# Five head norms summed in four row groups with their reciprocals spread by TensorE, and a new order in the attention loop

## The reference

```
def l2norm(t):                                    # DeltaNet q and k, 4 heads of 128 channels each
    return t * rsqrt(sum(t * t, axis=-1) + EPS)
y_dn = (rmsnorm(o_dn, onorm_g) * silu(z)) @ w_dn_out      # over the 128 channels of a head

def merge(r, m, rg, mo):                          # retention and mLSTM, 8 heads of 64 channels each
    r = _rmsnorm(r, ret_norm_w)   * silu(rg)
    m = _rmsnorm(m, mlstm_norm_w) * sigmoid(mo)
    return concatenate([r, m], axis=-1) @ w_out

k = _rmsnorm(_heads(k, 4), k_norm_w)              # attention keys, 4 heads of 64 channels
s_win = q @ k.T * scale       # 16 heads, query blocks of 128, window of 128 on both sides
s_ctx = q @ kc.T * scale      # all context keys
p = softmax([s_win, s_ctx] with one sink logit per head)
y = (p_win @ v + p_ctx @ vc) @ w_out
```

## Time and profile before

| | |
|---|---|
| median of 3 runs | 1986.92 us (1984.42 to 1987.09) |
| the profiled execution | 1981.02 us, of which the span of the trace is 1978.9 us |
| mean granted TensorE clock | 0.96 of full speed |
| PE busy | 1835.8 us (93%), 14672 matmuls |
| PEld busy | 1573.4 us (80%) |
| DVE busy | 918.0 us (46%), 1693 instructions |
| ACT busy | 759.8 us (38%), 1314 instructions |
| POOL busy | 462.2 us (23%), 226 instructions |
| DMA | 261.6 MB, mean 132 GB/s |

### The profile page before, as it was taken

One profiled execution on the slowest core, in us unless ns is written; L12 is line 12 of the kernel. 1 busy time (PEld: TensorE's weight loads), 2 busy tenths in 40 slices (PEclk: granted clock), 3 DMA queues, 4 the chain that ended last, 5 costly groups with the idle time before them and its releaser, 6 DMA issues.

```text
span 1978.9 us, 34373 instructions
## 1 busy us (share of the span) xinstructions
PE 1835.8 (93%) x14672; PEld 1573.4 (80%) x14672; DVE 918.0 (46%) x1693; ACT 759.8 (38%) x1314; POOL 462.2 (23%) x226
## 2 busy tenths in 40 slices
PE   5998999989799999998899969999999989999999
PEld 3777897877689998886687747888888767579998
DVE  1648626566443333435775664222232246744333
ACT  3454522332345454331533233322222234655443
POOL 0235212121123432121230001121212212013343
PEclk7999998999899999999998989999999999999999
DMA  8443344222365545312120023332332336134553
GB/s 319 163 160 128 107 150 150 88 108 87 128 249 186 188 171 184 110 69 96 64 86 23 22 106 108 148 106 107 107 128 107 106 139 228 71 118 181 181 182 128
DMA packets 36581, 261.58 MB, mean 132 GB/s; under 512 B 4048, under 2 KB 4176, under 8 KB 6224
## 3 DMA queue, kind: packets, MB, share of 16 engines
q1 hardware_dynamic: 36432, 259.40, 36.2%
HBM read 258.34 MB, written 1.05 MB: 131 GB/s over the span
## 4 chain that ended last, share of the span: by engine, by line
PE 79%; DVE 11%; ACT 4%; issue 3%; DMA 2%; POOL 1%; SPq 0%; DVEq 0%; ACTq 0%
PE ps L820 18%; PE ps L821 18%; PE ps L822 18%; PE ps L871 2%; PE ps L847 2%; PE ps L837 1%; DVE msq L2415 1%; PE ps L838 1%; PE ps L1089 1%; PE ps L839 1%; PE ps L1077 1%; PE ps L879 1%; PE ps L934 1%; PE ps L1095 1%; PE ps L1416 1%
## 5 line engine op out<-in xcount | busy, mean ns | idle before, releaser
L738 POOL TENSOR_TENSOR wl<-raw,wh 128x1024 fp32r<-128x1024 f32 (+1 forms) x179 | 427.2, 2389 | 1310.1 <-ACT wh L1458 1310.1
L820 PE MATMUL ps<-h_hi,wh 128*128 128x256 f32 (+1 forms) x1696 | 556.6, 328 | 6.9 <-POOL wl L738 4.7
L821 PE MATMUL ps<-h_lo,wh 128*128 128x256 f32 (+1 forms) x1696 | 548.5, 323 | 0.0
L822 PE MATMUL ps<-h_hi,wl 128*128 128x256 f32 (+1 forms) x1696 | 548.1, 323 | 0.0
L1458 ACT ACTIVATE wh<-raw 128x1024 fp32r<-128x1024 f32 (+1 forms) x330 | 342.1, 1040 | 399.9 <-PE ps L822 288.4
L820 PEld LDWEIGHTS ps<-h_hi,wh 128*128 128x128 f32 x1696 | 326.6, 193 | 36.5 <-POOL wl L738 8.9
L821 PEld LDWEIGHTS ps<-h_lo,wh 128*128 128x128 f32 x1696 | 326.4, 192 | 26.1 <-issue 2.7
L822 PEld LDWEIGHTS ps<-h_hi,wl 128*128 128x128 f32 x1696 | 326.4, 192 | 23.9
L1960 DVE TENSOR_TENSOR wl<-raw,wh 128x1024 fp32r<-128x1024 f32 (+1 forms) x151 | 188.1, 1245 | 242.8 <-ACT wh L1458 231.6
L820 PE MATMUL ps<-gh,wh 128*128 128x256 f32 (+1 forms) x528 | 169.3, 321 | 0.0
L822 PE MATMUL ps<-gh,wl 128*128 128x256 f32 (+1 forms) x528 | 168.2, 319 | 0.0
(11 more groups left out here) (414 smaller groups left out, 2741.7 us busy)
## 6 DMA issues: line engine op xcount, KB each, us to landing
raw<-in_mod SPq DMA_DIRECT2D x72, 1024.0 KB, 4.9
raw<-in_ffn_in SPq DMA_DIRECT2D x66, 1024.0 KB, 4.8
raw<-in_ffn_out SPq DMA_DIRECT2D x24, 1024.0 KB, 4.8
raw<-in_w_in SPq DMA_DIRECT2D x16, 1024.0 KB, 4.8
raw<-in_w_gate SPq DMA_DIRECT2D x12, 1024.0 KB, 4.9
raw<-in_w_ab SPq DMA_DIRECT2D x12, 1024.0 KB, 4.9
raw<-in_ffn_out SPq DMA_DIRECT2D x12, 768.0 KB, 4.2
raw<-in_w_at SPq DMA_DIRECT2D x5, 1024.0 KB, 4.8
```

Of the source, the lines that this page charges most:

```text
L738: nc.gpsimd.tensor_tensor(wl[e % SPLIT][:, 0:entries[e]["words"]], part(e), wh[e % SPLIT][:, 0:entries[e]["words"]].bitcast(F32), ALU.subt ...
L820: nc.tensor.matmul(b[:, cols], wh[e % SPLIT][:, w], xh(k), start=(k == 0), stop=False)
L821: nc.tensor.matmul(b[:, cols], wh[e % SPLIT][:, w], xl(k), start=False, stop=False)
L822: ins = nc.tensor.matmul(b[:, cols], wl[e % SPLIT][:, w], xh(k), start=False, stop=(k == nk - 1))
```

## The change

Head norms. `group_sums` replaces the matmul of 512 columns by four matmuls with a stationary matrix of 32 columns, each on 128 tokens, into four row groups (partitions 0 to 31, 32 to 63, ...) of columns 0 to 127 of one bank. Token 128 g + t then stands in column t of row group g. ACT's root and DVE's reciprocal work on 128x128. `group_spread` brings the reciprocals back to 128 x 512 with four matmuls of 128x128 (eight of 128x64 where a tile holds two heads), whose stationary operand is one column of the identity, broadcast, into a PSUM tile of its own (`l2s`, `osp`, `rsp`, `msp`, `aksp`); DVE's product reads it there. These 20 tiles are new in the plan. ACT's waits for `qk_ready`, `rout_ready` and `mout_ready` before a root or square go; PE gets waits for the reciprocals (`l2_inv`, `o_inv`, `rsp_inv`, `msp_inv`, `k_inv`), and where it used to wait for `qk_ready` it waits until `l2s` 7 is evacuated.

Attention loop. PE's order in a round is now transposes of u-1, outputs of u-2, scores of u+1, spread of u-1. `aol` is made by POOL; DVE waits for it before it overwrites `otmp`.

```
--- before.py
+++ after.py
+RETENTION_NORM = ((), (("rss", 0),), (("rss", 1), ("rsp", 0), ("rss", 2)), (("rsp", 1), ("rss", 3), ("rsp", 2)))
+MLSTM_NORM = ((("mss", 0), ("mss", 1), ("msp", 0)),
+              (("mss", 2), ("msp", 1), ("mss", 3), ("msp", 2), ("msp", 3)))
...
+        for w_ in range(16):                                             # POOL
+            pool.wait_ge(sem("ao_hi"), w_ + 1)
+            o = slice(P * (w_ % 2), P * (w_ % 2) + P)
+            nc.gpsimd.tensor_tensor(aol[:, w_ // 2, o], otmp[:, w_ % 2, :], aoh[:, w_ // 2, o].bitcast(F32),
+                                    ALU.subtract).then_inc(sem("ao_lo"), 1)
...
+        def group_sums(key, w, src):                                     # PE
+            b = begin(*key)
+            for g in range(4):
+                ins = nc.tensor.matmul(b[32 * g:32 * g + 32, 0:P], w, src[:, P * g:P * g + P], start=True, stop=True,
+                                       skip_group_check=True)
+            close(ins)
+        def group_spread(key, src, heads=1):
+            b = begin(*key)
+            for g in range(4):
+                rows = (slice(0, P),) if heads == 1 else HALF
+                for e, h in enumerate(rows):
+                    r = 32 * g + 16 * e
+                    ins = nc.tensor.matmul(b[h, P * g:P * g + P], ident[:, r:r + 1].to_broadcast([P, h.stop - h.start]),
+                                           src, start=True, stop=True)
+            close(ins)
...
-                        close(nc.tensor.matmul(begin("l2", m), CA("ones"), sqr[:, m % 2, :], start=True, stop=True))
+                        group_sums(("l2", m), CA("ones")[:, 0:32], sqr[:, m % 2, :])
+                        if m > 0:
+                            pe.wait_ge(sem("l2_inv"), m)
+                            group_spread(("l2s", m - 1), l2c[:, (m - 1) % 2, :])
...
-            b = begin("oss", i)
-            close(nc.tensor.matmul(b, CA("mean_128"), vbf(i), start=True, stop=True))
+            group_sums(("oss", i), CA("mean_128")[:, 0:32], vbf(i))
         for m in range(5, KD):
             hdense(("g0", m), LAT)
+            if m == 5:
+                for i in range(2):
+                    pe.wait_ge(sem("o_inv"), i + 1)
+                    group_spread(("osp", i), B["kd"][:, i, 0, :])
...
         for i in range(8):
             hdense(("aq", i), LAT)
+            if i == 0:
+                for z in range(2):
+                    pe.wait_ge(sem("k_inv"), z + 1)
+                    group_spread(("aksp", z), ars[:, z, 0:P], 2)
...
-                        if m >= 2:                                       # ACT, l2
-                            act.wait_ge(sem("qk_ready"), m - 1)
-                        free(A(l2r[:, m % 2, :], bank("l2", m), ACT.Sqrt, bias=eps), "l2", m)
+                        free(A(l2c[:, m % 2, :], bank("l2", m)[:, 0:P], ACT.Sqrt, bias=eps), "l2", m)
...
-                        act.wait_ge(sem(rdy), i - 1)                     # ACT, rss and mss
+                        full(act, ssname, i - 2)
...
         def l2norm(m):                                                   # DVE
-            evacuated(dve, "l2", m)
-            link(V.reciprocal(l2r[:, m % 2, :], l2r[:, m % 2, :]))
-            V.scalar_tensor_tensor(qk[:, m, :], qk[:, m, :], P ** -0.5 if m < 4 else 1.0, l2r[:, m % 2, :],
-                                   ALU.mult, ALU.mult).then_inc(sem("qk_ready"), 1)
+            if m < 8:
+                evacuated(dve, "l2", m)
+                V.reciprocal(l2c[:, m % 2, :], l2c[:, m % 2, :]).then_inc(sem("l2_inv"), 1)
+            if m > 0:
+                i = m - 1
+                full(dve, "l2s", i)
+                free(V.scalar_tensor_tensor(qk[:, i, :], qk[:, i, :], P ** -0.5 if i < 4 else 1.0, bank("l2s", i),
+                                            ALU.mult, ALU.mult), "l2s", i)
...
-        head_gain(mout, "mss", S("mn"), "mout_ready")
+        for i in range(5):
+            if i < 4:
+                head_root("mss", "msp", i)
+            if i > 0:
+                head_gain(mout, "msp", S("mn"), "mout_ready", i - 1)
...
-        for u in range(16 + 3):                                          # DVE, attention
+        for u in range(16 + 2):
...
-            if u >= 3:
-                w_ = u - 3
-                dve.wait_ge(sem("ao_hi"), w_ + 1)
-                o = slice(P * (w_ % 2), P * (w_ % 2) + P)
-                V.tensor_tensor(aol[:, w_ // 2, o], otmp[:, w_ % 2, :], aoh[:, w_ // 2, o].bitcast(F32),
-                                ALU.subtract).then_inc(sem("ao_lo"), 1)
...
+                if w_ >= 2:
+                    dve.wait_ge(sem("ao_lo"), w_ - 1)
                 free(V.tensor_tensor(otmp[:, w_ % 2, :], bank("ao", w_)[:, 0:P], rinv[:, w_ % 2, :], ALU.mult),
```

172 lines of the change are left out of this document (108 added, 64 removed).

## The result

| | before | changed |
|---|---|---|
| median | 1987.01 us (4 runs, 1984.42 to 1989.12) | 1969.92 us (4 runs, 1968.28 to 1974.38) |
| ratio | | 0.9918, 95% interval 0.9897 to 0.9939 |
| profiled execution / span | 1981.02 / 1978.9 us | 1968.28 / 1966.5 us |
| mean granted clock | 0.961 | 0.961 |

A forecast was written before the change was run, and what follows sets the result against it. PE was taken to bound most of the span (79% of the chain of waits), DVE 11%. Terms −11.5, −5.3, −6, −0.5, +1 and +1.2 sum to −21.1: 1959.9 us profiled, 1966 as median; whole range 1952 to 1982.

The forecast's parts named there:

- The sum, −21.1: Whole kernel: six stage terms together take 21.1 us off the profiled 1981.0, giving 1959.9, or 1966 as median.
- mLSTM norm, −11.5: mLSTM norm: shorter DVE reciprocals and fewer waits start `abo` 11.5 us sooner, PE's new work hidden; bounds −9 and −13.
- Loop, −5.3: Attention loop: round falls from 3.75 to 3.35 us, 0.40 over 13 full rounds, 5.3 us; bounds 0.5 and 7.2.
- The ring: Attention loop: scores, masking, reciprocal, spread, outputs, `otmp` wait on each other; outputs ahead of scores cut this, round 0.40 shorter.
- Retention, −6: Retention norm: PE's 6.98 us gap before `mv` nearly closes, then POOL's `wl` is late; 6 us less, bounds −2 and −8.
- l2, −0.5: l2 norms: PE's added work and one 1.7 us stall nearly cancel DVE's savings; −0.5 us, bounds −4 and +4.
- DeltaNet output +1: DeltaNet output norm: spreads hold PE some 4 us, mostly swallowed by old idle time; +1 us, bounds −1 and +4.
- keys +1.2: Attention keys: spreads wait for reciprocals behind DVE's `wl`; +1.2 us, bounds 0 and +2.5.
- PE's price of a tile, 0.65: All 20 norm tiles: PE pays 0.65 us more each, 0.15 of it for array-shape changes; 13 us; bounds 0 and 0.8.
- A: Rival, whole kernel: spreads are bare, PE's added work paid everywhere but the mLSTM norm; −7.5 us, or 1979; chance 0.2.
- B: Rival, attention loop: POOL's `aol` locks out DVE's small sums, round back to 3.75; total −15.8, 1971; chance 0.1.
- C: Rival, norms: late DVE reciprocals hold PE at the spreads, l2 +10; kernel +5 us slower, or 1992; chance 0.08.

The follow-up runs named there:

- the kernel with only the new order: Kernel before with only TensorE's new order in the attention loop, `aol` staying on DVE and the norms old; run once, 1977.44 us.
- the doubled spreads: Changed kernel with every matmul of the 20 spreads executed twice, the same result written again; run once, 1968.53 us.

## Why the prediction was right

**The sum, −21.1.** The six stages gave −16.0. That this is near is luck in part: the mLSTM norm gave 5.2 us less and the loop 1.3 less than forecast, and the retention norm 3.1 more, some 2 of which are the clock's.

**mLSTM norm, −11.5.** Measured −6.3. The mechanism was right: DVE's work fell by 9.8 us, and `abo` came sooner by 9.7 in two kernels. That the stage gained 11.1 and 11.0 there, near 11.5, is luck in part, since 1.4 of it is before's half clock behind the start of `abo`, which the forecast had kept for its bound of −13. The step said "PE has nothing else here, so all its new work is hidden". That sentence failed. In one of these kernels DVE waits 3.2 us inside the norm where 0.9 was counted, 1.9 of it for the third sum, which stands behind the modulation; and at half clock, spreads of 1.98 and modulation of 1.9 to 2.8 are no longer hidden behind a DVE that needs 2.35 per tile. I had counted the end of before's half clock as a possible gain ("−13") and not the half clock of the new kernel as a loss, though the scan's end has a wait of 2 us in both. That wait stands in the kernels with full clock there too, so what puts the half clock on the norm in one profile and not in another stays open.

**Loop, −5.3.** (13 × 0.40 is 5.2.) Measured −4.0, and by the order alone. The ring was cut as said, PE is the bound as said, but a round is 3.48 and not 3.35. The term that was mis-sized is PE's own: the spread takes 0.37 where it took 0.27, the outputs 1.02 where they took 0.97 and the transposes 1.03 where 1.0 was counted, less 0.08 for scores of 1.06 in place of 1.14. Spread and outputs, both with 64 stationary columns, no longer stand side by side, and I had taken both from the old neighbours; that this is why they take longer is read from the durations and was not tested by itself. 13 × 0.13 = 1.7 us too much, of which the loop's ends gave back 0.4. That `aol` would cost nothing was right; that it brings nothing either I had put as "DVE's 2.75", which bound nothing.

**Retention, −6.** Measured −8.3 to −9.1 in all seven profiles with these norms and single spreads: just outside the bound of −8. Against the kernel with only the new order, which lacks the half clock at 949.6 too, it is −7.4 for the changed kernel, inside it. Mechanism right; next late was nothing (L858 follows the spread at once), where I had left room for POOL's `wl`.

**l2, −0.5.** Measured −0.6, with one stall of 2.15 at the tile that was named by its cause. But −2.4 in the kernels in which no half clock followed the stall, and −1.9 to +1.1 with the old norms: that the number was met says little.

**DeltaNet output +1, keys +1.2.** Measured +1.6 and +2.4 in the first profile. In the four other profiles with the same code in these stages and single spreads the output norm gave +1.4 to +3.1 and the keys +0.1 to +1.5. Both stalls stood where they were put; at the output the spreads were ready earlier than in the forecast (2.32 us of wait for some 4), and the load followed 1.5 later (525.76 after 524.25), near the +1 that I had said.

**PE's price of a tile, 0.65.** The l2 pair went from 6.61 to 7.18: 0.57.

**Rivals.** A (bare spreads) is right for l2, output and keys, where the doubled spreads show it in full, and mostly for retention (2.8 us of some 3.7); it is wrong in what it made of the gain, 3 us for retention and 0.5 for the loop where 9.1 and 4.0 were measured. B (POOL holds DVE) is refuted: the round is 3.48 us with `aol` on DVE (only TensorE's order) and on POOL alike, and in the trace `aol` runs from 1704.30 to 1704.76 while DVE masks from PSUM, and the DVE operations with two SBUF operands (1705.06 on) come later. The lock that the Trainium skill describes (SBUF — State Buffer, "SBUF: two separate sides") thus had nothing to act on here, while in the l2 stage the trace agrees with it once more: 2.48 us for a convolution product, 0.49 without POOL. C was right about the place, one stall at the l2 reciprocals and one at the output, and 2 us each in place of 7 and 4.

The Trainium skill, TensorEngine Tiling (Array Packing), Key Properties, says that changing the tiling mode drains TensorE. The loop's trace agrees in that the spread lets the next matmul begin after 0.37 us with another shape behind it and after 0.27 with its own; no run here isolates the drain, and none shows the 0.15 us that the prediction added per tile. I had weighed it against the norms and not against the loop.

## What to carry to other kernels

A long DVE operation on a result that is the same in all partitions is worth folding into row groups when DVE ends the waits around it; TensorE pays about 0.6 us per tile for it, so place each spread where TensorE would not wait, behind more work of its own and with the reciprocal early in DVE's order (3.8, 2.4 and 1.0 us in three stages, 1.8 of it half clock). When an engine's order is rearranged, price its matmuls with their new neighbours. When the forecast empties one engine, work out the new bound at half clock as well.

## What the runs showed of the hardware

The same kernel's profiled spans were 1966.5 and 1981.2 us at mean granted clocks of 0.961 and 0.952, and a kernel with some 18 us more TensorE work (an estimate: 20 tiles with 0.9 each, as in the l2 stage) took the same 1968.5 us at 0.971. Where TensorE is the bound and its code unchanged, stretches moved by 2 to 7 us from one profile to the next. So an edit of under 4 us was read from its stage only, and compared between stages with the same granted clock.
